# Head norm summed by token column, part of the second output unit's work moved, unread products at seams: a one-core decoder step on Trainium2

## The reference, cut to what matters

```python
def finish_diff_heads(o, g_subln, lam_init):          # o: (b, t, 4 heads, 128)
    o = rms_norm(o, g_subln) * (1.0 - lam_init)       # mean square over the 128 of one head and token
    return o.reshape(o.shape[0], o.shape[1], ATTN_WIDTH)

def merge_groups(attn_o, ssm_y, w_glu, g_ssm_out, w_out):
    y = jax.nn.gelu(ssm_y)
    y = y * jax.nn.sigmoid(y @ w_glu)
    y = rms_norm(y, g_ssm_out)
    return jnp.concatenate([attn_o, y.astype(attn_o.dtype)], axis=-1) @ w_out

# in the layer
y = y + rms_norm(merge_groups(att, ssm_y, ...), g_mix_post)                 # mixer
y = y + rms_norm(mem_attend(rms_norm(y, g_mem_pre), mk, mv, w_mq, w_mo), g_mem_post)
y = y + rms_norm(swiglu(rms_norm(y, g_ffn_pre), w_gate, w_up, w_down), g_ffn_post)
```

## Time and profile before

| | us |
|---|---|
| runs | 999.61, 995.48, 996.18 |
| median | 996.18 |
| the profiled execution, own time | 998.68 |
| its span | 996.9 |
| outside the span | 1.8 |
| PE busy | 935.8 (94%) |
| DVE busy | 451.8 (45%) |
| ACT busy | 359.0 (36%) |
| POOL busy | 179.4 (18%) |

### The profile page before, as it was taken

The page is one execution under the profiler, slowest core; times in us unless marked ns, Lnnn a source line. Parts: engine busy times, 40 slices in busy tenths (PEclk is TensorE's granted clock), DMA queues, the critical chain, the costliest instruction groups (busy, mean ns, idle before and its releaser), DMA issues.

```text
span 996.9 us, 17892 instructions
## 1 busy us (share of the span) xinstructions
PE 935.8 (94%) x7616; PEld 867.1 (87%) x7616; DVE 451.8 (45%) x900; ACT 359.0 (36%) x565; POOL 179.4 (18%) x45
## 2 busy tenths in 40 slices
PE   3989988898899999999889989999999999999997
PEld 2989987765589998985469989999999999999996
DVE  5798975675544677111554492222232222101113
ACT  5432223675453464225434453222222222122111
POOL 3000000000000001300033001344443333343330
PEclk9999999789999999999999899999999999999999
DMA  8304205422242257539051102222222232222212
GB/s 220 102 30 128 86 1 208 155 85 86 77 140 85 85 169 254 211 144 396 10 169 43 43 1 85 84 84 84 84 84 84 85 100 97 87 75 74 85 32 90
DMA packets 85342, 105.84 MB, mean 106 GB/s; under 512 B 9473, under 2 KB 72834, under 8 KB 85154
## 3 DMA queue, kind: packets, MB, share of 16 engines
q1 hardware_dynamic: 85056, 104.92, 31.6%
q10 hardware_dynamic: 226, 0.05, 0.0%
HBM read 98.26 MB, written 6.70 MB: 105 GB/s over the span
## 4 chain that ended last, share of the span: by engine, by line
PE 81%; DVE 9%; ACT 5%; issue 3%; DMA 1%; POOL 1%; ACTq 0%; DVEq 0%
PE pall L1782 56%; PE pall L1794 6%; PE pall L1819 3%; PE pall L2104 2%; PE pall L2146 1%; ACT w_hi L662 1%; PE pall L2157 1%; PE pall L1974 1%; PE pall L1871 1%; DVE w_lo L1100 1%; PE pall L1854 1%; PE pall L1875 1%; PE pall L1806 1%; PE pall L1965 1%; PE pall L2193 1%
## 5 line engine op out<-in xcount | busy, mean ns | idle before, releaser
L623 POOL TENSOR_TENSOR w_lo<-w_raw,w_hi 128x2048 fp32r<-128x2048 f32 (+1 forms) x38 | 171.3, 4508 | 777.0 <-DVE w_lo L1100 371.7
L1782 PE MATMUL pall<-x_hi,w_hi 128*128 128x272 f32 x1024 | 213.9, 290 | 1.0 <-issue 1.0
L1782 PE MATMUL pall<-x_lo,w_hi 128*128 128x272 f32 x1024 | 212.3, 289 | 0.0
L1782 PE MATMUL pall<-x_hi,w_lo 128*128 128x272 f32 x1024 | 211.0, 287 | 0.0
L1782 PEld LDWEIGHTS pall<-x_hi,w_hi 128*128 128x128 f32 x1024 | 160.8, 189 | 2.1 <-issue 1.4
L1782 PEld LDWEIGHTS pall<-x_lo,w_hi 128*128 128x128 f32 x1024 | 161.8, 189 | 0.0
L1782 PEld LDWEIGHTS pall<-x_hi,w_lo 128*128 128x128 f32 x1024 | 161.0, 189 | 0.0
L662 ACT ACTIVATE w_hi<-w_raw 128x2048 fp32r<-128x2048 f32 (+1 forms) x61 | 114.7, 1880 | 91.3 <-PE pall L1782 91.2
L1782 PE MATMUL pall<-g_hi,w_hi 128*128 128x272 f32 x352 | 73.1, 289 | 0.0
L1782 PE MATMUL pall<-g_lo,w_hi 128*128 128x272 f32 x352 | 72.7, 288 | 0.0
L1782 PE MATMUL pall<-g_hi,w_lo 128*128 128x272 f32 x352 | 72.6, 287 | 0.0
(11 more groups left out here) (379 smaller groups left out, 1630.9 us busy)
## 6 DMA issues: line engine op xcount, KB each, us to landing
w_raw<-in_w_gate SPq DMA_DIRECT2D x10, 1024.0 KB, 5.4
w_raw<-in_w_up SPq DMA_DIRECT2D x10, 1024.0 KB, 5.4
w_raw<-in_w_in SPq DMA_DIRECT2D x8, 1024.0 KB, 6.5
w_raw<-in_w_down SPq DMA_DIRECT2D x8, 1024.0 KB, 4.9
dm_kv<-in_cache_mem_v SPq DMA_DIRECT2D x5, 1024.0 KB, 13.8
w_raw<-in_w_out SPq DMA_DIRECT2D x4, 1024.0 KB, 8.5
d_k<-in_cache_k SPq DMA_DIRECT2D x16, 256.0 KB, 3.3
d_v<-in_cache_v SPq DMA_DIRECT2D x16, 256.0 KB, 4.3
```

The lines of the kernel that those rows point to most:

```text
L623: e.tensor_tensor(w_lo[:, n % 2, 0:w], w_raw[:, n % 2, 0:w], w_hi[:, n % 2, 0:w].bitcast(F32), ALU.subtract)\
L1782: ins = mm(acc(j)[:, a, :], w, x[:, k_x + k, a * HALF:(a + 1) * HALF], start=first and k == 0 and s_, stop=last and k == kts - 1 and t_)
```

## The change

**Heads' norm by token column.** ACT squares each prompt head straight from bank 5 right after copying it to `oT`, into `sq_head` (two 128x512 tiles). `head_sums(h)` on PE takes 128 token columns of it as the stationary operand and one column of ones as the moving one: four products of one column per head, so that a token's sum lands on its own partition. They stand in steps 9, 11 and 15 for heads 0, 1 and 2 (`hsum`). `hsumd` has ACT load the square root's table ahead, and square the decode columns of the four heads at once. Root and reciprocal are then of 16 + 4 columns (`h_root`) instead of 128x544. The broadcast along partitions is a product of that column, broadcast to 128, with the identity (four of 128 columns and one of 32 per head).

**Output unit 0's S5 half** is cut: the first 128 output rows whole in step 16, the other 128 in two quarters, between which the last head's sums and the decode sums stand.

**Second output unit.** ACT makes its `w_hi` in step 12 instead of step 6; DVE makes its `w_lo` after the norm's last low part instead of ahead of the reciprocal.

**Memory output.** The `w_lo` of the third and fourth MO unit moves from POOL to DVE. The square root's table for norm n3 is loaded after the evacuation of half 11. The second half's `sum_half` moves from ahead of the first feed-forward product to ahead of its record k = 3, and `add_half(15)` moves one `low_half` earlier.

**Unread products** are added in nine places (10 before `b_pad`, 6 before each of two S5 state steps, 7 before the scores of block 1, 6 before `dkt 4`, 5 at n1, 5 and 5 at n2, 4 each before the last two `m_p` transposes, 5 each before the last two `dot`s), 68 in all; 8 of 12 go from the last two attention blocks, and the 6 of the heads' norm.

```diff
@@ order
-               9: [("do", 0), ("dot", 0), ("dks", 1)], 10: [("dsm", 1)], 11: [("dsc", 1), ("dpt", 1)], 12: [("dpe", 1), ("dv", 1)],
-               13: [("do", 1)], 14: [("dot", 1)]}
+               9: [("do", 0), ("dot", 0), ("dks", 1), ("hsum", 0)], 10: [("dsm", 1)], 11: [("dsc", 1), ("dpt", 1), ("hsum", 1)], 12: [("dpe", 1), ("dv", 1), ("out_hi", 0)],
+               13: [("do", 1)], 14: [("dot", 1)], 15: [("hsum", 2)],
+               16: [("out_s5", 0)]}
...
-    order += [("attv", NH - 1), ("subln", 0)]
+    order += [("hsumd", 0), ("attv", NH - 1), ("subln", 0)]
@@ POOL
-        for n in range(U_MQ + 1, U_FFN):
+        for n in range(U_MQ + 1, U_MO + 2):
@@ ACT
-                e.activation(oT[:, n, 0:NP_TOK], bank(5), ACT.Copy).then_inc(S("att_oT"), 1)
+                e.activation(oT[:, n, 0:NP_TOK], bank(5), ACT.Copy)
+                if n >= 2:
+                    e.wait_ge(S("subln_sum"), n - 1)
+                e.activation(sq_head[n % 2][:], bank(5), ACT.Square, scale=P ** -0.5).then_inc(S("att_oT"), 1)
...
-                for h in range(NH):
-                    if h >= 2:
-                        e.wait_ge(S("subln_sum"), h - 1)
-                    e.activation(sq[:, h % 2, :], oT[:, h, :], ACT.Square, scale=P ** -0.5).then_inc(S("subln_sq"), 1)
...
-                e.activation(two(rstd[:]), halves(4), ACT.Sqrt, bias=small[:, EPS_COL:EPS_COL + 1]).then_inc(S("subln_root"), 1)
+                e.wait_ge(S("subln_sum"), NH + 1)
+                e.activation(h_root[:, 0:16], bank(7)[:, 320:336], ACT.Sqrt, bias=small[:, EPS_COL:EPS_COL + 1]).then_inc(S("subln_root"), 1)
...
-                if n == SF - 1:
-                    hi_ahead(U_OUT + 1)
+            elif kind == "out_hi":
+                hi_ahead(U_OUT + 1)
...
+            elif i == 11:
+                e.activation(small[:, 60:61], small[:, EPS_COL:EPS_COL + 1], ACT.Sqrt)
@@ DVE
-                split_lo()
-                e.wait_ge(S("subln_root"), 1)
-                e.reciprocal(rstd[:], rstd[:]).then_inc(S("subln_r"), 1)
+                e.wait_ge(S("subln_root"), 2)
+                e.reciprocal(h_root[:, 0:16], h_root[:, 0:16]).then_inc(S("subln_r"), 1)
...
                 low(NH - 1)
+                split_lo()
...
+            if i == 5:
+                e.wait_ge(w_lo_ready, U_MO + 2)
+                split_lo()
+            elif i == 7:
                 split_lo_first(0)
+                split_lo()
@@ PE
             if f >= 2:
+                keep_busy(bank(4), 6)
                 e.wait_ge(S("yssm"), f - 1)
...
-            if n >= len(ATT) - 2:
-                keep_busy(bank(2), 6)
+            if n == len(ATT) - 1:
+                keep_busy(bank(2), 4)
...
+        def head_sums(h):
+            e.wait_ge(S("att_oT"), h + 1)
+            for c in range(4):
+                ins = mm(bank(7)[:, 320 + 4 * h + c:321 + 4 * h + c], sq_head[h % 2][:, c * P:(c + 1) * P], ones[:, 0:1], start=True, stop=True)
+            ins.then_inc(S("subln_sum"), 1)
+
+        def out_s5(m, k, kts):
+            product(J_OUT + m, U_OUT % 2, 256, m * P, ssm_hi, ssm_lo, k, kts, k == 0, False, k_off=4 + k)
...
             elif kind == "mats_b":
-                e.wait_ge(S("b_pad"), 2 * (n + 1))
...
+                else:
+                    keep_busy(bank(4), 10)
+                e.wait_ge(S("b_pad"), 2 * (n + 1))
...
             elif kind == "att":
+                if n == 1:
+                    keep_busy(bank(2), 7)
...
                 elif n == 4:
+                    keep_busy(bank(3), 6)
                     e.wait_ge(S("rstd_half"), 1)
...
             elif kind == "subln":
-                e.wait_ge(S("dT_out"), 2)
-                keep_busy(bank(4), 6)
+                out_s5(1, 0, 2)
+                head_sums(3)
...
+                out_s5(1, 2, 2)
+                e.wait_ge(S("subln_r"), 2)
...
+            elif kind == "out_s5":
+                e.wait_ge(w_lo_ready, U_OUT + 1)
+                e.wait_ge(*counted("ssmn", "lo", SF))
+                e.wait_ge(S("att_biased"), len(ATT))
+                out_s5(0, 0, 4)
...
         e.wait_ge(S("mn_lo"), KT)
+        keep_busy(bank(6), 5)
         e.wait_ge(*counted("n1", "add", KT - 1))
...
+        keep_busy(bank(6), 5)
         e.wait_ge(*counted("n2", "add", KT - 1))
         spread_sum("n2")
+        e.wait_ge(S("xT_out"), KT)
+        keep_busy(bank(4), 5)
...
         def ma_tail(n):
-            e.wait_ge(S("ma_p"), n + 1)
             if n >= 1:
                 e.wait_ge(S("ma_pTo"), n)
+            if n >= len(MATT) - 2:
+                keep_busy(bank(6), 4)
+            e.wait_ge(S("ma_p"), n + 1)
...
             elif kind == "dot":
+                if n >= 2:
+                    e.wait_ge(S("ma_pTo"), 13 + n // 3)
+                    keep_busy(bank(6), 5)
...
-        sum_half(bank(5), "n3", 1)
...
+                if (i, k) == (0, 3):
+                    sum_half(bank(5), "n3", 1)
```

47 lines of the change are left out of this document (23 added, 24 removed).

## The result

The changed kernel took 992.35 us, the median of 6 runs (991.23 to 994.06), against 995.41 us for the kernel before (6 runs, 995.09 to 999.61). The ratio is 0.9945 with a 95% interval of 0.9923 to 0.9967: a gain of 3 us where 13 were forecast, and outside the range of 978.0 to 990.5. The profiled execution of the changed kernel took 994.06 against 998.68, 4.6 less where the sum had said 14.7.

The account below looks back on a forecast made before the run. PE was taken to bound the kernel (81% of the page's chain), with gaps and half clock; terms summed to -14.7 from the profiled 998.7, giving 984.0 (981.5 against the median); median put at 983.0, range 978 to 990.5.

Parts of the forecast that it names:

- clock terms: Gains from PE keeping full clock: 1.6 before b_pad, 1.1 + 1.0 at block 1, 1.1 at key transposes, 3.1 at n3.
- heads' norm: From values product to end of out 0: 0.9 + 4.95 + 7.18 = 13.0 against 19.57 us, -6.6, bounds -4.5 and -8.
- steps 6 to 14: Four one-column products per head, 0.33 a head for two heads in dense stretches: +0.4 us, bounds 0 and +1.
- part before b_pad and S5 states: Unread products under waits: -1.6 us before b_pad if they hold the clock, +0.2 in the S5 states.
- Scores of block 1: Seven unread products under a 1.85 us wait; gated unit starts earlier and at full clock: -2.2 us, bounds 0 and -2.5.
- Key transposes: Six unread products, 1.5 under a 1.55 us wait; stretch to 213.0 at full clock: -1.1 us, 0 to -1.5.
- rival 4: Slower: unread products meet PE at half clock, 0.47 instead of 0.25 us each; 1009 for the execution, median 1006; chance 0.03.
- Norms n1 and n2: 15 unread products, 3.75 us, under waits for DVE's additions of about 1 us each and more: +0.2, 0 to +1.5.
- End of the memory attention: 18 unread products, 4.5 us, in a row with ACT's copies; values product later: +2.8 us, bounds +0.9 and +3.5.
- Memory output: Low parts moved from POOL to DVE remove 1.9 us of PE waiting in two gaps: -1.9, bounds -0.5 and -2.
- Norm n3, first half: Root's table loaded ahead saves 1.3 us, then the clock holds for 3.1: -4.4, bounds -1.3 and -4.6.
- Norm n3, second half: With the sum behind the first products, these start when the low parts are there: -0.5 us, 0 to -1.

Follow-up runs that it names:

- second profile of before: The kernel before, unchanged, executed and profiled once more: 994.81 us.
- the norm alone: Kernel before with only the heads' norm by token columns, S5 halves and moved split of the second output unit: median 996.11 us, ratio 0.9987.
- MO and n3 alone: Kernel before with only the last two memory output units' low parts on DVE and the root's table loaded ahead for n3: 994.20 us, ratio 0.996.

## Why the prediction was wrong, point by point

**The clock terms and the base.** "The sum is made against the profiled execution's own 998.7 us", and "the changed kernel has fewer places for it", for a falling clock: these two steps failed. The clock terms were 1.6, 1.1 + 1.0, 1.1 and 3.1, 7.9 of the 14.7 us. That execution had 35.9 us at half clock; of the 49 later runs of the kernel before, 25 took 997 us or less. And a fall kept off in one place did not lower the total: the mean half-clock time is 25.4 against 30 to 33, some 5 to 7 us less and worth about 3, and it is 24.4 without the added unread products, so what was saved is not theirs. The text saw that falls differ between executions and answered by taking 1 us off; it should have booked the clock terms at 0 to full and let the waits alone make the sum. These come to -6.8. The clock-free number fell by 2.3, from 982.0 to 979.7: most of the rest is missing in the heads' norm, 2.9 where 6.2 were forecast with steps 6 to 14.

**The part before b_pad and S5 states, -1.4.** -1.0 in the profile, but not by the terms alone. Of the lead of 1.7 the wait for b_pad took back 1.1; the held clock then gave 1.6 and the two S5 seams cost 0.2, both as forecast; 0.8 went at 86 us and 0.2 later, where no part of the change stands. In five of eight profiles without the seam the clock is at 1.00 there anyway, so the 1.6 can be won only in some executions.

**Scores of block 1, -2.2.** -2.4 in the profile, with the mechanism as told: the gated unit starts behind y_lo. The second profile of before has the whole of it without the change.

**Key transposes, -1.1.** 0. The clock fell ahead of the seam, in the S5 norm's broadcasts, so the unread products ran at half-clock price. Changed kernel:

```profile
199.83 3.06 PE L2100 MATMUL pall<-ident,small 68*128 68x68 f32 x16
202.68 2.87 PE L1821 MATMUL pall<-ident 128*128 128x128 f32 x12
```

2.87 for six products under a wait of 1.55. This is rival 4 in one place: "the clock has to be at half when they start". A fall ahead of a seam was held unlikely from one profile, where it came at 206.2; in eleven of the thirteen later profiles of all kernels, the second one of before among them, it lies between 199.5 and 201.6, ahead of the key transposes. As to the Trainium skill's rule on transposes, TensorE: Matmul & The Clock Gate, Part 4: PE-mode transpose, the runs neither need it nor show it: the 3.3 us at 176, mostly transposes, held 1.00 in one execution and 0.53 in another of one kernel.

**Steps 6 to 14, +0.4.** +1.5, and the same in the profile of the norm alone. A term that I sized wrongly: 8 records are four products, not eight (`sum_half` too has four products, not the eight that its description gives), and the row I priced them by has a stationary side of 68 columns, these have 128.

```profile
258.43 1.05 PE L1908 MATMUL pall<-ones,sq_head 128*128 128x1 f32 x8
```

Next start 0.91 later, so 0.9 a head instead of 0.33. Two heads stand in dense stretches.

**The heads' norm, -6.6.** -3.4, and -4.9 where step 16 kept its clock. The mechanism held: the reciprocal of 3.55 became one of 0.25 and the wide sums are gone. The sum's three terms, 0.9 + 4.95 + 7.18, came out as 2.4 + 5.8 + 7.7. The first is a half-clock stretch of 3.4 us in step 16's S5 products, worth 1.5, behind a gap of 0.94 that the new wait for the last scores makes; in the profile of the norm alone this term is 0.9. The others are products priced too low. PE and DVE of the changed kernel:

```profile
272.42 0.95 PE L1908 MATMUL pall<-ones,sq_head 128*128 128x1 f32 x8
273.30 0.41 PE L2061 MATMUL pall<-ones,sq_dec 128*32 128x1 f32 x8
273.64 0.52 PE L1797 MATMUL pall<-ssm_hi,w_hi 128*128 128x272 f32 x2
...
275.25 1.05 PE L2070 MATMUL pall<-ident,h_root 128*128 128x128 f32 x8
276.23 0.40 PE L2071 MATMUL pall<-ident,h_root 32*128 32x32 f32 x2
276.57 1.16 PE L2070 MATMUL pall<-ident,h_root 128*128 128x128 f32 x8
...
276.67 0.72 DVE L1103 TENSOR_TENSOR tt<-oT,pall 128x544 f32<-128x544 f32 x1 [2.20 <-PE pall L2071]
278.09 0.72 DVE L1103 TENSOR_TENSOR tt<-oT,pall 128x544 f32<-128x544 f32 x1 [0.70 <-PE pall L2071]
```

The values product ends at 270.8, so the first multiplication comes 5.8 us behind it. The one-column sums of the last head and of the decode columns take 1.2 where 0.65 was forecast, eight products read as four from the same row as above, and the first head's broadcasts take 1.4 where 1.1 was forecast. The second multiplication now waits 0.70 for PE, where before the two ran back to back: 7.7 to the end of out 0 at 284.4, where 7.18 was taken as unchanged. "From there DVE's chain is as before" failed by 0.5. The split of the second output unit, at 283.4, cost nothing, as forecast.

**Norms n1 and n2, +0.2.** No shift. The +1.7 in the table's line at 487 is a fall of the clock in the memory attention, where the change has nothing.

**End of the memory attention, +2.8.** +2.9, and 2.6 to 3.4 back when taken out. Right in mechanism and size. "No fall of the clock followed there, so nothing is won" rested on one execution: in three of the ten profiles without these products it did fall there, at 504 to 507, and took 3.1 in one.

**Memory output, -1.9.** -2.4 in the profile; in the second profile of before against MO and n3 alone -2.5. Right: all of it falls at the two products that had waited for POOL's low part, 1.5 at the first. Not foreseen is that POOL's split also held DVE. Before, POOL and DVE:

```profile
537.09 4.58 POOL L623 TENSOR_TENSOR w_lo<-w_raw,w_hi 128x2048 fp32r<-128x2048 f32 x1 [21.21 <-ACT w_hi L662]
537.87 4.10 DVE L1097 TENSOR_TENSOR sqacc<-sqacc,q_half 128x272 f32<-128x272 f32 x1 [2.50 <-ACT q_half L986]
```

The addition that starts beside the split takes 4.10 and ends 0.3 after it; alone, in the changed kernel, the same one takes 0.43. No wait of PE ended with it.

**Norm n3, first half, -4.4.** -4.4 in the profile. 1.3 of it is a wait that every profile has. The rest is the clock: all four profiles with the old root load have a fall there, but it is 6.8 us long in one and 3.4 in three, so about 1.5 of the 3.1 can be counted on.

**Norm n3, second half, -0.5.** +2.4, beyond the bound of 0. "a new fall in the thin stretch is in the 0" was the failing step: a fall there doesn't last for the thin records only but for the dense products after them too, 573 to 582.8. It was 11.6 us long on average in the five profiles with the moved sum and no filling, against 4.4 in the seven with the sum in its old place; at 0.45 a us these 7.2 us are worth 3.2, an estimate that covers the 2.9 missed.

## What to carry to other kernels

When a kernel's PE drops to half clock in places, take two profiles of it before booking any clock gain, and keep the sum of waits and the sum of clock terms apart: the waits repeated to some tenths here (but for the one at b_pad, 1.57 to 2.49, which hangs on how early the start reaches full pace), the clock did not. Before calling a seam useful or useless, look both at its place and at the total: here no fall stood behind the seams at b_pad and block 1 in any of six profiles, and the time at half clock was not lower. Unread products belong only under a wait that they cannot lengthen; between a copy and the transposes that reuse its bank they add to the path, 2.9 us for 18 of them. A wait that moves behind a few early products is not shorter if what releases those behind it is another engine's chain.

## What the runs showed of the hardware

One kernel's executions differed by up to 9 us (991.1 to 999.9) with identical instructions, and the mean granted clock (0.990 to 0.978) goes with it: the same wait of 1.85 or 1.86 us before block 1 was followed by half clock in three profiles and not in five. Others were the same each time: gaps of 1.89 at n3's root and of 3.0 to 3.2 at its second sum were followed by a fall in 4 of 4 and 7 of 7 profiles, and the S5 norm, with a gap of only 0.64 ahead in most, in 14 of 14. A gap of 0.94 in step 16 and of 0.80 before were enough too. A fall can go on through dense work: 573 to 582.8 in the changed kernel. Clock held in one place did not lower the total, since stretches at half clock turned up in others. An addition of 128x272 float32 on DVE took 4.10 us instead of 0.43 beside POOL's split. A product with a 128x128 float32 stationary side and one column costs about 0.23 us in a row of them, nearly as much as one of 128 columns (0.25).
